# The last gated MLP's first product by Strassen's scheme

## The reference, cut to what matters

```python
h = layer_norm_3(ALPHA * h + mix, ln1_g[l], ln1_b[l])
gate, up = jnp.split(h @ w_gate_up, 2, axis=-1)       # 1024 x 1024 times 1024 x 5632
ffn = (jax.nn.silu(gate) * up) @ w_down               # 1024 x 2816 times 2816 x 1024
h = layer_norm_3(ALPHA * h + ffn, ln2_g[l], ln2_b[l])
```

## Time and profile before

| | us |
|---|---|
| median of 3 runs | 3232.83 (3230.95 to 3234.42) |
| the profiled execution | 3231.26 |
| its span | 3229.9 |
| TensorE busy | 3061.9 |
| VectorE busy | 1594.6 |
| ScalarE busy | 1075.7 |

### The profile page before, as it was taken

How to read it: one execution, slowest core, us unless ns; L and a number is a source line. 1 busy time by engine, 2 the same in 40 slices (tenths; PEclk the granted TensorE clock), 3 DMA queues, 4 the chain that set the end, 5 groups by cost and what they waited for, 6 DMA issues and landing times.

```text
span 3229.9 us, 33639 instructions
## 1 busy us (share of the span) xinstructions
PE 3061.9 (95%) x14238; PEld 2402.3 (74%) x14238; DVE 1594.6 (49%) x2166; ACT 1075.7 (33%) x1523; POOL 2.2 (0%) x6
## 2 busy tenths in 40 slices
PE   7999899999999998999997989999798999999997
PEld 5887677888888876777765857665486888888884
DVE  4442336444544446776674454667745333333335
ACT  3223423222212224445447254555624111111113
POOL 0000000000000000000000000000000000000000
PEclk9999899999999999999999999999799999999998
DMA  3211011111111111111100101010010111111111
GB/s 135 82 58 36 30 47 45 46 46 50 52 49 46 46 46 40 33 39 39 33 26 21 45 26 33 20 33 18 17 40 29 50 46 53 46 47 52 49 50 52
DMA packets 48820, 141.60 MB, mean 44 GB/s; under 512 B 12790, under 2 KB 16670, under 8 KB 48542
## 3 DMA queue, kind: packets, MB, share of 16 engines
q1 hardware_dynamic: 48670, 139.45, 13.8%
HBM read 135.16 MB, written 9.77 MB: 45 GB/s over the span
## 4 chain that ended last, share of the span: by engine, by line
PE 87%; ACT 5%; DVE 4%; issue 3%; DMA 0%; SPq 0%; ACTq 0%; DVEq 0%
PE psum L444 59%; PE psum L826 10%; PE psum L478 5%; PE psum L500 2%; PE psum L489 2%; PE psum L753 1%; PE psum L736 1%; PE psum L908 1%; PE psum L935 1%; PE psum L495 1%; ACT sb_left L1621 1%; DVE swa_p L2346 0%; PE psum L653 0%; ACT sb_pt L1633 0%; ACT w_hi L1020 0%
## 5 line engine op out<-in xcount | busy, mean ns | idle before, releaser
L444 PE MATMUL psum<-h_hi,w_hi 128*128 128x512 f32 x2080 | 645.9, 392 | 6.6 <-ACT ret_q L1113 2.9
L444 PE MATMUL psum<-h_lo,w_hi 128*128 128x512 f32 x2080 | 641.3, 389 | 0.0
L444 PE MATMUL psum<-h_hi,w_lo 128*128 128x512 f32 x2080 | 641.1, 389 | 0.0
L1732 DVE TENSOR_TENSOR w_lo<-w_raw,w_hi 128x1024 fp32r<-128x1024 f32 x228 | 278.6, 1222 | 424.8 <-ACT w_hi L1020 424.4
L444 PEld LDWEIGHTS psum<-h_hi,w_hi 128*128 128x128 f32 x2080 | 389.4, 188 | 92.3 <-issue 13.0
L444 PEld LDWEIGHTS psum<-h_lo,w_hi 128*128 128x128 f32 x2080 | 390.7, 188 | 81.6
L444 PEld LDWEIGHTS psum<-h_hi,w_lo 128*128 128x128 f32 x2080 | 390.7, 188 | 81.5
L1020 ACT ACTIVATE w_hi<-w_raw 128x1024 fp32r<-128x1024 f32 x228 | 239.7, 1052 | 412.3 <-PE psum L444 369.5
L1973 DVE TENSOR_TENSOR residual<-residual,psum 128x1024 f32<-128x1024 f32 x176 | 214.6, 1219 | 170.3 <-PE psum L444 169.3
L444 PE MATMUL psum<-mlp_act_hi,w_hi 128*128 128x512 f32 x704 | 219.7, 394 | 12.8 <-DVE mlp_act_lo L1979 11.3
L444 PE MATMUL psum<-mlp_act_hi,w_lo 128*128 128x512 f32 x704 | 218.5, 392 | 0.0
(11 more groups left out here) (280 smaller groups left out, 3467.5 us busy)
## 6 DMA issues: line engine op xcount, KB each, us to landing
w_raw<-in_weights SPq DMA_DIRECT2D x228, 512.0 KB, 3.5
residual<-in_x_t SPq DMA_DIRECT2D x8, 512.0 KB, 8.7
out_t<-residual SPq DMA_DIRECT2D x8, 512.0 KB, 3.0
rel_copies<-rel_rows SPq DMA_DIRECT2D x8, 480.0 KB, 5.6
na_bias<-rel_copies SPq DMA_DIRECT2D x8, 240.0 KB, 4.1
band_copies<-band_rows SPq DMA_DIRECT2D x8, 192.0 KB, 6.1
ret_rotary<-in_rotary SPq DMA_DIRECT2D x1, 1024.0 KB, 7.8
swa_bias<-band_copies SPq DMA_DIRECT2D x4, 256.0 KB, 2.7
```

What stands on the lines that cost most here:

```text
L444: ins = self.pe.matmul(out[:, s], w[:, k, at:at + P], src(k, low)[:, s], start=(k == 0 and part == 0), stop=(k == n_k - 1 and part == 2))
L1732: self.dve.tensor_tensor(self.m.w_lo[:, n % 2, :], self.m.raw[:, n % 2, :], self.m.w_hi[:, n % 2, :].bitcast(F32), ALU.subtract).then_inc( ...
```

## The change

The first product of channel tiles 1 to 21 is computed as a 2x2 by 2x2 product of blocks with seven multiplications in place of eight. The input is cut into channel halves (k 0 to 3 and 4 to 7) and token halves; the weights into gate and up, and channel halves. Each of the seven products is half channels by half tokens: 4 k x 3 parts = 12 matmuls into one bank. Four banks take seven products: the first four start a bank, the last three are added to what an earlier one left there, after that was read.

- **Input.** Once per MLP VectorE makes three combinations T of the input's quarters from the kept input (12 half tiles), ScalarE their high parts, VectorE their low parts; a fourth combination then takes the place of a quarter of `h_hi` and `h_lo`.
- **Weights.** Four of the seven weight parts are sums of the gate's and up's halves, made on VectorE (`block_sums`). The high and low parts go by blocks of 128x512 in a ring of four (`block_high`, `block_low`, two blocks ahead); the down tiles go in the same blocks. Raw slots come free by `raw_free`: a gate tile's at its last low part G2, an up tile's at U2, a down tile's at its second half.
- **Outputs.** ScalarE copies the first product and takes two silus of half a tile, VectorE adds up the rest (`products`).
- **Order.** The second product of a group runs between the two channel tiles of the next; in the last group the four outputs of the first tile take their first 24 matmuls from hidden tile 20, before tile 21 is waited for.
- The wait of VectorE for the last kept input (`act_l2_keep`) goes; `l2_bias` is moved in memory.

```diff
@@ the order of stages and of half tiles of weights ("blocks")
+class Plan:
+    G1, S2, S3, S1, G2, U2, S4 = range(7)
...
+        self.stages = [("up", 1)]
+        for g in range(1, NGROUP):
+            self.stages += [("up", 2 * g), ("down", g - 1), ("up", 2 * g + 1)]
+        self.stages.append(("down", NGROUP - 1))
...
+            if kind == "up":
+                self.blocks += [("up", i, j) for j in range(7)]
+            else:
+                self.blocks += [("down", self.d[2 * i + half], j) for half in range(2) for j in range(2)]
@@ Memory.block_source: the sources of the seven weight parts of a channel tile
+        g, u = self.raw[:, plan.a[i] % 2, :], self.raw[:, plan.b[i] % 2, :]
+        return (g[:, 0:HALF], self.wsum[1], u[:, 0:HALF], self.wsum[0], g[:, HALF:S], u[:, HALF:S], self.wsum[1])[j]
@@ TensorProgram: self.mlp(MLP3, "l2", False) becomes self.strassen(PLAN3, "l2")
+    def strassen(self, plan, norm):
...
+        for kind, i in plan.stages:
+            if kind == "up":
+                self.seven(plan, i)
+            elif i < NGROUP - 1:
+                self.second(plan, i)
+            else:
+                self.last_second(plan, i)
+    def seven(self, plan, c):
...
+        moving = ((x11(m.h_hi), x11(m.h_lo)), t[1], t[2], t[0], (x21(m.h_hi), x21(m.h_lo)), (x12(m.h_hi), x12(m.h_lo)),
+                  (x22(m.h_hi), x22(m.h_lo)))
+        needed = ((), ("dve_t_lo" + name, 3, 1), ("dve_t_lo" + name, 3, 2), ("dve_t_lo" + name, 3, 0), (), ("dve_t_lo" + name, 3, 3), ())
+        bank = (0, 1, 2, 3, 0, 2, 3)
+        emptied = (("act_c11" + name, c), ("dve_u2" + name, c), ("dve_c21" + name, c), ("dve_c12" + name, c))
+        read = {4: ("act_s1" + name, c), 5: ("dve_u3" + name, c), 6: ("dve_c22" + name, c)}
+        for j in range(7):
+            if j < 4:
+                out.append(self.take(("ms_" + name, c, j), j, 1, emptied[j]))
+            else:
+                q.wait_ge(*on(*read[j]))
+            if needed[j]:
+                q.wait_ge(*on(*needed[j]))
+            q.wait_ge(*on("mw_lo_" + name, first + j))
+            w_hi, w_lo = (m.block(buf, first + j).rearrange("p (k n) -> p k n", n=P) for buf in (m.w_hi, m.w_lo))
+            high, low = moving[j]
+            for k in range(4):
+                for part, (w, x) in enumerate(((w_hi, high), (w_lo, high), (w_hi, low))):
+                    ins = self.pe.matmul(out[bank[j]], w[:, k, :], x(k), start=(j < 4 and k == 0 and part == 0),
+                                         stop=(k == 3 and part == 2), skip_group_check=True)
+            ins.then_inc(*self.to("ms_" + name, c, j))
+    def last_second(self, plan, g):
...
+        for k in range(2):
+            self.q.wait_ge(*self.on("dve_hid_lo" + plan.name, 2 * g + k))
+            for n in range(4):
+                if k == 0:
+                    outs.append(self.take(("down", t, n), (4, 6, 0, 2)[n], 2, ("dve_down", t, n)))
+                ins = self.second_part(plan, g, 0, n, k, outs[n])
...
@@ ScalarProgram.mlp3
+        for k in range(4):
+            for i, src in ((2, self.t_temp(k, 0)), (0, self.t_temp(k, 1)), (1, m.t2_keep[k])):
+                q.wait_ge(*on("dve_t_summlp3", k, i))
+                act.activation(m.t_hi[i][:, k, :], src, ACT.Copy, scale=1.0 / ALPHA).then_inc(*to("act_t_himlp3", k, i))
+        self.block_high(plan, 0)
+        q.wait_ge(*on("proj", plan.a[0]))
+        act.activation(m.ta[:], m.place["proj", plan.a[0]], ACT.Silu).then_inc(*to("act_gatemlp3", 0))
+        self.block_high(plan, 1)
+        self.block_high(plan, 2)
+        self.hidden_high(plan, 0)
+        self.block_high(plan, 3)
+        for k in range(4):
+            q.wait_ge(*on("dve_t_summlp3", k, 3))
+            act.activation(m.h_hi[:, k, HALF:S], m.t2_keep[k], ACT.Copy, scale=1.0 / ALPHA).then_inc(*to("act_t_himlp3", k, 3))
+        for n in range(1, len(plan.blocks) + 1):
+            if 4 <= n + 2 < len(plan.blocks):
+                self.block_high(plan, n + 2)
+            kind, c, j = plan.blocks[n - 1]
+            if kind == "up" and j == 0:
+                q.wait_ge(*on("ms_mlp3", c, 0))
+                if c == 1:
+                    q.wait_ge(*on("dve_t_lomlp3", 3, 1))
+                else:
+                    q.wait_ge(*on("dve_c12mlp3", c - 1))
+                act.activation(m.us, m.place["ms_mlp3", c, 0], ACT.Copy).then_inc(*to("act_s1mlp3", c))
+                if c > 1 and c % 2 == 0:
+                    self.hidden_high(plan, c - 1)
+            elif kind == "up" and j == 4:
+                q.wait_ge(*on("ms_mlp3", c, 4))
+                q.wait_ge(*on("dve_mmlp3", c - 1, *((0,) if c > 1 else ())))
+                act.activation(m.ta[:, 0:HALF], m.place["ms_mlp3", c, 0], ACT.Silu).then_inc(*to("act_c11mlp3", c))
+            elif kind == "up" and j == 6:
+                q.wait_ge(*on("dve_c12mlp3", c))
+                act.activation(m.ta[:, HALF:S], m.ta[:, HALF:S], ACT.Silu).then_inc(*to("act_c12mlp3", c))
+                if c == 2 * NGROUP - 1:
+                    self.hidden_high(plan, c)
...
@@ VectorProgram.mlp3
+        for k in range(5):
+            if k < 4:
+                x1, x2 = m.x[:, k, :], m.x[:, k + 4, :]
+                t3, t1 = ((m.us, m.vs), (m.tp[:, 0:HALF], m.tp[:, HALF:S]))[k % 2]
+                q.wait_ge(*on("act_l2_keep", k + 4))
+                if k >= 2:
+                    self.after("dve_t_lomlp3", k - 2, 1)
+                dve.tensor_tensor(t3, x2[:, HALF:S], x1[:, HALF:S], ALU.subtract).then_inc(*to("dve_t_summlp3", k, 2))
+                dve.tensor_tensor(t1, x1[:, HALF:S], x1[:, 0:HALF], ALU.subtract).then_inc(*to("dve_t_summlp3", k, 0))
+                self.after("dve_t_summlp3", k, 0)
+                dve.tensor_tensor(m.t2_keep[k], x2[:, HALF:S], t1, ALU.subtract).then_inc(*to("dve_t_summlp3", k, 1))
+            if k:
+                t3, t1 = ((m.us, m.vs), (m.tp[:, 0:HALF], m.tp[:, HALF:S]))[(k - 1) % 2]
+                for i, src in ((2, t3), (0, t1), (1, m.t2_keep[k - 1])):
+                    q.wait_ge(*on("act_t_himlp3", k - 1, i))
+                    dve.scalar_tensor_tensor(m.t_lo[i][:, k - 1, :], src, 1.0 / ALPHA, m.t_hi[i][:, k - 1, :].bitcast(F32), ALU.mult,
+                                             ALU.subtract).then_inc(*to("dve_t_lomlp3", k - 1, i))
+        self.block_sums(plan, 0)
+        self.block_sums(plan, 1)
+        self.block_low(plan, 0)
+        self.block_low(plan, 1)
+        self.block_sums(plan, 2)
+        q.wait_ge(*on("act_gatemlp3", 0))
+        q.wait_ge(*on("proj", plan.b[0]))
+        dve.tensor_tensor(m.tp[:], m.ta[:], m.place["proj", plan.b[0]], ALU.mult).then_inc(*to("dve_mmlp3", 0))
+        self.block_low(plan, 2)
+        self.hidden("mlp3", 0)
+        self.block_sums(plan, 3)
+        self.block_low(plan, 3)
...
+                dve.tensor_tensor(m.t2_keep[k], m.x[:, k + 4, 0:HALF], m.t2_keep[k], ALU.subtract).then_inc(*to("dve_t_summlp3", k, 3))
...
+        for n in range(1, len(plan.blocks) + 1):
+            ahead = 4 <= n + 2 < len(plan.blocks)
+            if ahead:
+                self.block_sums(plan, n + 2)
+            kind, c, j = plan.blocks[n - 1]
+            if kind == "up":
+                self.products(plan, c, j)
+                if j == 6 and c == 2 * NGROUP - 1:
+                    self.hidden("mlp3", c)
...
+            if ahead:
+                self.block_low(plan, n + 2)
+            if kind == "up" and j == 0 and c > 1 and c % 2 == 0:
+                self.hidden("mlp3", c - 1)
...
+    def products(self, plan, c, j):
...
+        if j == 1:
+            q.wait_ge(*on("act_s1" + name, c))
+            dve.tensor_tensor(m.us, m.us, bank[1], ALU.add).then_inc(*to("dve_u2" + name, c))
+        elif j == 2:
+            self.after("dve_u2" + name, c)
+            if c > 1:
+                self.after("dve_m" + name, c - 1, 1)
+            dve.tensor_tensor(m.vs, m.us, bank[2], ALU.add).then_inc(*to("dve_u3" + name, c))
+        elif j == 3:
+            self.after("dve_u3" + name, c)
+            dve.tensor_tensor(m.vs, m.vs, bank[3], ALU.add).then_inc(*to("dve_c22" + name, c))
+        elif j == 5:
+            self.after("dve_hid_lo" + name, c - 1)
+            dve.tensor_tensor(both[0], m.us, bank[2], ALU.add).then_inc(*to("dve_c21" + name, c))
+            self.after("dve_c21" + name, c)
+            q.wait_ge(*on("act_c11" + name, c))
+            dve.tensor_tensor(both[0], both[0], gate[0], ALU.mult).then_inc(*to("dve_m" + name, c, 0))
+        elif j == 6:
+            dve.tensor_tensor(gate[1], m.us, bank[3], ALU.add).then_inc(*to("dve_c12" + name, c))
+            self.after("dve_c22" + name, c)
+            q.wait_ge(*on("act_c12" + name, c))
+            dve.tensor_tensor(both[1], gate[1], m.vs, ALU.mult).then_inc(*to("dve_m" + name, c, 1))
+    def block_sums(self, plan, n):
...
+        if j == plan.S2:
+            q.wait_ge(*on(f"w_loaded{plan.a[i] % 2}", plan.a[i]))
```

(50 more changed lines are left out.)

155 lines of the change are left out of this document (115 added, 40 removed).

## The result

The changed kernel takes 3180.27 us (median of 4 runs, 3179.78 to 3180.48) against 3232.66 for the kernel before: a ratio of 0.9837, 95% interval 0.9823 to 0.9850, or 52.4 us less. The forecast was 3182.

A forecast was written before the change was run, and what follows sets the result against it. The prediction took the last MLP to cost what its TensorE matmuls cost. Its terms, -57.1 + 10.4 + 3.0 - 6.5 = -50.2 us, gave 3181.1 from the profiled execution, 3182.7 by the median; forecast 3182, range 3172 to 3200.

The forecast's parts named there:

- 252 matmuls less: Channel tiles 1 to 21 take 84 matmuls each, not 96, at an unchanged 0.2267 us: -57.1 us.
- wait at the start: After the pair, TensorE waits for VectorE's input combinations and the first product's low weights: +10.4 us.
- half clock after it: First matmuls following TensorE's new wait run at half clock: +3.0 us, ends 0 and 6.
- the end: Last group: 24 matmuls using only the tile before remove the wait and clock fall; -6.7, with 0.2 allowed: -6.5 us.
- the tail: What follows the last group's work was taken as unchanged: 0 us.
- Rival C: Weights loaded for each matmul no longer hidden: step 0.32 us, +171 us, so 3353; chance 0.02.
- the bank's part of A: Twelve matmuls adding into one bank double the excess per matmul, +23 us; within a 3191 to 3205 rival, chance 0.13.
- The bound of +23 us: Upper end for matmuls adding into one bank: 1764 x 0.0133 us, if the bank doubled the step's excess.
- The Trainium skill's rule: VectorE's next op doesn't start until the pipe is empty; steps at the start longer, +2.2 us, time 3184.
- It holds by 0.5 us: First channel tile by seven products: low(4) ready at 2510.4 for a start at 2510.9; otherwise up to 3 us.
- The stages: Between the ends, VectorE's 13.1 us of work per channel tile hides in 19.0 us: no waits, 0 us.
- rival B: VectorE two blocks late, three products per tile wait for bank reads: 88 us, 3270; chance 0.03.

The follow-up runs named there:

- seven products from tile 2 on: Channel tile 1 computed the old way with 96 matmuls, input combinations made beside it, against the changed kernel; 3169.90 us.
- The filled start: Changed kernel plus 44 matmuls of 128x512, result unread, in TensorE's wait after the pair; 3181.00 us.
- one block: Changed kernel with high and low parts of a block, and its sum, made one block ahead and not two; 3200.96 us.
- the old order: Changed kernel with the last group's second product taking both hidden tiles at once, so starting when hidden tile 21 is done; 3186.44 us.
- 7 and 14 more on VectorE: Changed kernel plus one, or two further, unread 128x512 VectorE instructions after each product; 3186.14 us with 7 more per channel tile, 3218.68 us with 14.
- Filling its waits: Filler matmuls after the pair, plus 12 unread matmuls before the last norm's mean and 8 behind it, against the changed kernel; 3180.57 us.

## Why the prediction was right

By its own steps, with the terms as the profiles before and after give them:

| step | forecast | measured | from |
|---|---|---|---|
| 252 matmuls less | -57.1 | -57.1 | 38.08/168 = 0.2267 a step |
| wait at the start | +10.4 | +10.4 | 2488.70 to 2499.14 |
| half clock after it | +3.0 | +2.4 | 40.52 - 38.08 |
| the end | -6.5 | -6.5 | last product to mean: 31.0 before, 24.5 after |
| the tail | 0 | -1.4 | 37.1 before, 35.6 after |
| ahead of the MLP | 0 | +1.6 | scaling starts at 2461.17 before, at 2462.76 after |
| sum | -50.2 | -50.6 | span: -50.7 |

- **Matmuls.** Neither the one bank for twelve in a row nor the own weights cost anything: the timeline has 0.23 us from each to the next. Rival C falls, and the bank's part of A. The bound of +23 us was much too wide.
- **The start.** That the term was right to 0.1 us is luck: small errors cancel in it. The scalar_tensor_tensor of 128x512 follows in 0.60 us, not 0.67 (twelve of them, -0.8); the 0.67 was read from an instruction with a scalar per partition, busy for 0.75 us where these are busy for 0.69. Against that, two waits of VectorE for its own earlier low parts (k - 2) cost 0.2 each, which the count had not; 0.15 pass from the end of the weights' low part (2498.99) to the first matmul; and TensorE was free 0.2 earlier than taken, since the timeline before has the next tile's first matmul at 2487.12 where the chain says 2487.28. Taking the wait away by order alone (seven products from tile 2 on) gave the 10 us that the two terms say, so the cause is shown.
- **The Trainium skill's rule** in VectorE: DVE Perf Modes, The DRAIN you can't avoid: the steps at the start, 0.60 to 0.61 us between instructions busy for 0.69, are again shorter than the sentence that the prediction took from it allows. But the prediction had left out how that paragraph ends, that a next instruction starts earlier where it is not held back. The steps here agree with this end, so they do not speak against the section as a whole. The forecast by the rule was 3184; it had also lengthened five steps that wait for a result and are 0.72 already.
- **The products behind it.** "It holds by 0.5 us" was close: the fifth product's low part ended at 2511.47 and the product began at 2512.31, 0.8 later. The filled start confirms how little that is: TensorE was 2.4 us earlier, and 1.6 to 1.8 of them were waited for there.
- **The stages.** No wait at all, VectorE busy for 63% (60 to 66 forecast). 4.2 us more work per tile still costs none there, 9.2 us cost 3.06 a group of two tiles. So waiting for VectorE begins somewhere between 17.3 and 22.3 us of its work per tile, and at 22.3 it is 1.5 us per tile: less than the forecast had for rival B, 2.4 us at 21.4. It also stands in another place than any that the prediction named, the banks of the down stage. One step of the prediction was wrong and did not show: it took product 0 of an even tile for the longest iteration, with the next low part there after 1.3 us. After product 6 that takes longer, since the output sum, ScalarE's silu and the product stand in front: in the changed kernel product 6 of tile 3 ends at about 2580.5 and that low part at 2583.25, 2.8 us later. The second block of lead, 5.4 us in all, covers it; one block, 2.7, did not.
- **The end.** Shown by the old order: 4.6 us of waiting and 2.6 at half clock come back, and 6.9 in the median.
- **The tail** was called unchanged and was not: before, the granted clock was 0.77 over 5 us of the last norm and 30 sums took 14.70 us; after, it stayed full and they took 13.16. The tables by stretch, before and after:

```profile
3199.70:3204.70 5.00, 5.00 (x10) 2.15 (x9) 5.00 (x6) 1.86 (x3) 0.00 (x0) 0.77 0.00 0
```

```profile
3150.40:3155.40 5.00, 5.00 (x13) 2.14 (x12) 5.00 (x6) 2.74 (x4) 0.00 (x0) 1.00 0.00 0
```

This does not come with the seven products as such. With nothing changed in it, the last norm's sums took 13.16 us in four of the other kernels run here (the changed kernel again, seven products from tile 2 on, the old end, one block ahead) and 14.76 to 14.78 in three (the filled start, 7 and 14 more on VectorE). Filling its waits brought 14.76 back to 13.16. Which idle stretch lowers the clock in a given kernel stays open.

The median moved by 52.4 and the span by 50.7: the profiled execution before was 1.4 us under its median, the one after 0.2 over. Of the 2.4 us between the sum's 3182.7 and the measured 3180.27, 1.8 are thus the step from the profiled execution to the median and 0.6 the terms of the table, in which -1.4 of the tail and +1.6 ahead of the MLP, neither forecast, cancel by luck.

## What to carry to other kernels

Where TensorE is busy for all of a stage, count matmuls by the measured step and then look only at the stage's two ends: here they cost 12.8 us at the start and gave back 6.5 at the end, against 57.1 from the matmuls. Work that must be ready before a new scheme can start belongs beside matmuls of the old scheme, even if those are dearer: 2.7 us of extra matmuls hid 12.8. And idle time on an engine is not slack by itself: with the order of the list as it is, one block less of lead cost 21 us, though VectorE was busy for less than two thirds of the stages.

## What the runs showed that I had not expected

- The last norm costs 1.6 us more or less with TensorE's granted clock (13.16 us or 14.70 to 14.78 for the same 30 matmuls), and up to 3.4 with its mean (3.7 to 5.4 us for 8). Both profiles of the changed kernel have the same times, and kernels with nothing changed there differ, so it can pass for the effect of an edit.
- TensorE kept at full clock by filler matmuls saved 2.4 us on the first product, and the kernel gained nothing: up to 1.8 went in a wait for VectorE four products later, and the rest in the last norm's clock.
